# A two-layer block kernel: the rotary half-swap made by a TensorE matmul instead of by DMAs

## The reference, cut to what matters

```python
def apply_rope(x, cos, sin):
    x1, x2 = jnp.split(x.astype(jnp.float32), 2, axis=-1)
    c = cos[None, :, None, :]
    s = sin[None, :, None, :]
    return jnp.concatenate([x1 * c - x2 * s, x1 * s + x2 * c], axis=-1).astype(x.dtype)
```

## Time and profile before

| | us |
|---|---|
| median of 3 runs | 2912.36 (2909.82 to 2913.0) |
| the profiled execution, its own time | 2913.0 |
| its span, first to last instruction | 2911.2 |
| PE busy | 2748.0 (94%) |
| DVE busy | 1624.0 (56%) |
| ACT busy | 1092.4 (38%) |
| POOL busy | 608.6 (21%) |

### The profile page before, as it was taken

How to read it: one execution, slowest core, us unless ns; L and a number is a source line. 1 busy time by engine, 2 the same in 40 slices (tenths; PEclk the granted TensorE clock), 3 DMA queues, 4 the chain that set the end, 5 groups by cost and what they waited for, 6 DMA issues and landing times.

```text
span 2911.2 us, 36239 instructions
## 1 busy us (share of the span) xinstructions
PE 2748.0 (94%) x14752; PEld 2138.2 (73%) x14752; DVE 1624.0 (56%) x2752; ACT 1092.4 (38%) x1788; POOL 608.6 (21%) x338
## 2 busy tenths in 40 slices
PE   6999889999999998999998999989998999989997
PEld 5877568878878676788886888656676888756675
DVE  5779655554467674665456477744415247744424
ACT  3233633323232454433223563244313473244312
POOL 0000025776700000455450141000110131000110
PEclk8999989999999998999999999999999999999999
DMA  7353024454522111344442444211222223221222
GB/s 233 103 165 100 28 87 144 145 173 133 178 86 66 58 56 58 116 146 144 130 145 87 138 140 120 65 62 44 80 80 92 87 68 113 69 69 44 73 87 73
DMA packets 307462, 297.30 MB, mean 102 GB/s; under 512 B 9184, under 2 KB 300128, under 8 KB 307296
## 3 DMA queue, kind: packets, MB, share of 16 engines
q1 hardware_dynamic: 306048, 289.01, 31.6%
q0 software_dynamic: 960, 5.51, 0.5%
q10 hardware_dynamic: 288, 0.47, 0.0%
HBM read 284.73 MB, written 2.10 MB: 99 GB/s over the span
## 4 chain that ended last, share of the span: by engine, by line
PE 84%; DVE 6%; ACT 5%; POOL 2%; DMA 2%; issue 1%; DVEq 0%; ACTq 0%; SPq 0%; POOLq 0%
PE ps L516 83%; PE ps L699 2%; DVE wl L1266 1%; POOL raw L1729 1%; DMA raw<-in_w_in 1%; ACT wh L857 1%; DVE hl L1272 1%; DMA raw<-in_w_up 1%; DVE uv L1272 1%; POOL raw L1732 1%; POOL ug L1705 0%; DVE s L1528 0%; ACT recat L857 0%; DVE rawt L1272 0%; ACT s L857 0%
## 5 line engine op out<-in xcount | busy, mean ns | idle before, releaser
L516 PE MATMUL ps<-hh,wh 128*128 128x512 f32 x2288 | 933.0, 408 | 38.9 <-DVE hl L1272 26.1
L516 PE MATMUL ps<-hh,wl 128*128 128x512 f32 x2288 | 901.1, 394 | 0.0
L516 PE MATMUL ps<-hl,wh 128*128 128x512 f32 x2288 | 900.6, 394 | 0.0
L1266 DVE TENSOR_TENSOR wl<-raw,wh 128x2048 fp32r<-128x2048 f32 (+2 forms) x186 | 444.2, 2388 | 358.5 <-ACT wh L857 358.0
L516 PEld LDWEIGHTS ps<-hh,wh 128*128 128x128 f32 x2288 | 434.1, 190 | 166.9 <-issue 62.3
L516 PEld LDWEIGHTS ps<-hh,wl 128*128 128x128 f32 x2288 | 434.0, 190 | 95.9
L516 PEld LDWEIGHTS ps<-hl,wh 128*128 128x128 f32 x2288 | 435.2, 190 | 87.2 <-issue 4.3
L857 ACT ACTIVATE wh<-raw 128x2048 fp32r<-128x2048 f32 (+2 forms) x186 | 342.5, 1842 | 252.8 <-PE ps L516 134.1
L1729 POOL TENSOR_TENSOR raw<-raw,cond 128x2048 f32<-128x2048 f32 x40 | 182.2, 4555 | 252.5 <-DMA raw<-in_w_ada 252.5
L857 ACT ACTIVATE rawt<-ps 128x512 f32<-128x512 f32 (+1 forms) x106 | 63.3, 598 | 323.9 <-PE ps L516 323.8
L1732 POOL TENSOR_TENSOR raw<-raw 128x1024 f32<-128x1024 f32 x80 | 168.6, 2107 | 6.3
(11 more groups left out here) (229 smaller groups left out, 3812.8 us busy)
## 6 DMA issues: line engine op xcount, KB each, us to landing
raw<-in_w_in SPq DMA_DIRECT2D x74, 1024.0 KB, 5.5
raw<-in_w_ada SPq DMA_DIRECT2D x64, 1024.0 KB, 5.3
raw<-in_w_up SPq DMA_DIRECT2D x44, 1024.0 KB, 5.3
raw<-in_w_in SPq DMA_DIRECT2D x44, 512.0 KB, 5.1
raw<-in_w_out SPq DMA_DIRECT2D x16, 1024.0 KB, 5.4
raw<-in_w_down SPq DMA_DIRECT2D x16, 1024.0 KB, 5.4
stage<-in_w_ada SPq DMA_DIRECT2D x8, 1024.0 KB, 11.4
t1s<-rawt SPq DMA_DIRECT2D x124, 64.0 KB, 2.0
```

The costliest lines, as they stand in the source:

```text
L516: return e.matmul(o, a, b, start=start, stop=stop, skip_group_check=True)
L1266: return e.tensor_tensor(o, a, b, op)
```

## The change

The swap becomes a matmul with a constant 128x128 matrix of 0, 1 and -1. `rest` becomes a unit of PE too: it takes a bank of the main pool, waits for ACT's copy in `rawt`, and multiplies. The four DMAs of a tile and their waits on SP are gone, so that SP's program is a plain list of loads. POOL's product with `cos` now goes into `t1s`; DVE's product with `sin` reads the new PSUM bank and writes the destination, and the add follows. The constants grow by 128 columns (64 KB). The planner's table says that `rest` costs 0.9 on PE and then 1.4 on DVE, and this moves other work, as shown below the diff.

```diff
-C_ID, C_ONE, C_BLK, C_NTRI, C_NONE, C_CAUS, C_SWA, C_COS, C_SIN = (
-    0, 128, 256, 384, 512, 640, 768, 1024, 1536)
-C_W = 2048
+C_ID, C_ONE, C_BLK, C_ROT, C_NTRI, C_NONE, C_CAUS, C_SWA, C_COS, C_SIN = (
+    0, 128, 256, 384, 512, 640, 768, 896, 1152, 1664)
+C_W = 2176
...
-    "rope": (("ACT", 0.7, True), ("POOL", 1.3, False)), "rest": (("DVE", 1.5, True),), "v2": (("ACT", 0.4, True),),
+    "rope": (("ACT", 0.7, True), ("POOL", 1.3, False)), "rest": (("PE", 0.9, True), ("DVE", 1.4, True)), "v2": (("ACT", 0.4, True),),
...
-IN_MAIN_BANK = ("z", "q", "iv", "g", "qk", "a", "cqk", "v2", "rope", "bv", "gate", "mg", "br", "iw", "bvt")
+IN_MAIN_BANK = ("z", "q", "iv", "g", "qk", "a", "cqk", "v2", "rope", "bv", "gate", "mg", "br", "rest", "iw", "bvt")
...
-        elif unit[0] in ("iw", "bvt"):
+        elif unit[0] in ("rest", "iw", "bvt"):
...
+    def rest(l, nm, c):
+        dst, r = rope_of(M, nm, c)
+        b = take("main", ("rest", l, nm, c))
+        go.wait_ge(*at("rope_raw", l, nm, c))
+        mm(b[r, :], M.rot[r, r], M.rawt[X.slot["rope", l, nm, c]][r, :], True, True).then_inc(*up("pe_rest", ("rest", l, nm, c)))
...
-        raw_slot(("rope", l, nm, c), ("rope_cos", l, nm, c), ("rope_turned", l, nm, c))
+        raw_slot(("rope", l, nm, c), ("rope_cos", l, nm, c), ("rest", l, nm, c))
...
     def rest(l, nm, c):
         dst, r = rope_of(M, nm, c)
-        turned = M.t1s[X.slot.get(("rope", l, nm, c), 0)][r, :]
-        go.wait_ge(*at("rope_turned", l, nm, c))
-        tt(turned, turned, M.sin[r, :], ALU.mult).then_inc(*up("dve_rope"))
+        b, t1 = bank("rest", l, nm, c), M.t1s[X.slot.get(("rope", l, nm, c), 0)]
+        go.wait_ge(*at("rest", l, nm, c))
+        if nm == "bk":
+            go.wait_ge(*at("ts", l, 3, 3))
+        tt(dst, b[r, :], M.sin[r, :], ALU.mult).then_inc(*up("dve_rope", ("out", ("rest", l, nm, c))))
         go.wait_ge(*last("dve_rope"))
         go.wait_ge(*at("rope_cos", l, nm, c))
-        tt(dst, dst, turned, ALU.add).then_inc(*up("dve_rope", ("roped", l, nm, c), (
+        tt(dst, dst, t1[r, :], ALU.add).then_inc(*up("dve_rope", ("roped", l, nm, c), (
...
-        if nm == "bk":
-            go.wait_ge(*at("ts", l, 3, 3))
-        e.tensor_tensor(dst, M.rawt[X.slot.get(("rope", l, nm, c), 0)][r, :], M.cos[r, :], ALU.mult).then_inc(
-            *up("pool_rope", ("rope_cos", l, nm, c)))
+        if t1_free[n] is not None:
+            go.wait_ge(*at(*t1_free[n]))
+        t1_free[n] = ("roped", l, nm, c)
+        e.tensor_tensor(M.t1s[n][r, :], M.rawt[n][r, :], M.cos[r, :], ALU.mult).then_inc(*up("pool_rope", ("rope_cos", l, nm, c)))
...
-        for to in range(r.start, r.stop, 32):
-            src = to + 32 if to % 64 == 0 else to - 32
-            e.dma_start(M.t1s[n][to:to + 32, :], M.rawt[n][src:src + 32, :]).then_inc(*up16(f"turned_in{n}", ("rope_turned", l, nm, c)))
```

More of the change, by code:

```diff
@@ L147, in __init__ @@
         self.blk = cst[:, C_BLK:C_BLK + 128]
+        self.rot = cst[:, C_ROT:C_ROT + 128]
         self.caus = cst[:, C_CAUS:C_CAUS + 128]
@@ L1705, in up_value @@
         e.tensor_tensor(M.ug[ch % 4][:, :], M.ug[ch % 4][:, :], M.uv[ch % 3][:, :], ALU.mult).then_inc(*up("pool_gate", ("gated_f", l, ch)))
+    t1_free = [None, None]
     def rope(l, nm, c, c0, n, j):
[L1708 removed]
+        r = rope_of(M, nm, c)[1]
+        n = X.slot.get(("rope", l, nm, c), 0)
         go.wait_ge(*at("rope_raw", l, nm, c))
[L1710 to L1713 removed]
+        if t1_free[n] is not None:
+            go.wait_ge(*at(*t1_free[n]))
+        t1_free[n] = ("roped", l, nm, c)
+        e.tensor_tensor(M.t1s[n][r, :], M.rawt[n][r, :], M.cos[r, :], ALU.mult).then_inc(*up("pool_rope", ("rope_cos", l, nm, c)))
     def c_low(l, c, u):
@@ L1760, in sync_program @@
     M, T, up16, at, go, plan = X.M, X.T, X.tally.up16, X.tally.at, Go(e), X.plan
-    turned_free = [None, None]
     def first(n0, n1):
@@ L1766, in first @@
                 *up16(f"stage_in{n}", ("stage", n)))
-    def load(j, p):
+    xv = T["xT"].rearrange("(k p) s -> p k s", p=128)
+    for k in range(0, KD, 2):
+        e.dma_start(M.xT[:, k:k + 2, :], xv[:, k:k + 2, :]).then_inc(*up16(f"x_in{k}", ("loaded", "x", k // 2)))
+    first(0, 2)
+    for j, p in enumerate(plan):
         if j == 2:
@@ L1782, in load @@
             e.dma_start(view(M.raw[i]), src).then_inc(*up16(f"raw_in{i}", ("raw", j)))
-    def rope(l, nm, c):
-        n, r = X.slot.get(("rope", l, nm, c), 0), rope_of(M, nm, c)[1]
-        go.wait_ge(*at("rope_raw", l, nm, c))
-        if turned_free[n] is not None:
-            go.wait_ge(*at(*turned_free[n]))
-        turned_free[n] = ("roped", l, nm, c)
-        for to in range(r.start, r.stop, 32):
-            src = to + 32 if to % 64 == 0 else to - 32
-            e.dma_start(M.t1s[n][to:to + 32, :], M.rawt[n][src:src + 32, :]).then_inc(*up16(f"turned_in{n}", ("rope_turned", l, nm, c)))
-    xv = T["xT"].rearrange("(k p) s -> p k s", p=128)
-    for k in range(0, KD, 2):
-        e.dma_start(M.xT[:, k:k + 2, :], xv[:, k:k + 2, :]).then_inc(*up16(f"x_in{k}", ("loaded", "x", k // 2)))
-    first(0, 2)
-    loads, free = list(enumerate(plan)), {None}
-    while loads and loads[0][1]["raw_before"] in free:
-        load(*loads.pop(0))
-    for kind, *rest_ in X.order:
-        if kind == "rope":
-            rope(*rest_[:3])
-        elif kind in ("split", "ada", "adap") or kind == "br" and rest_[2] % 2:
-            free.add(rest_[-1])
-            while loads and loads[0][1]["raw_before"] in free:
-                load(*loads.pop(0))
     ov = X.out.rearrange("(k p) s -> p k s", p=128)
@@ L2286, in constants @@
     c[:, C_BLK:C_BLK + 128] = (i[:, None] // 64 == i[None, :] // 64)
+    r = np.zeros((128, 128), np.float32)
+    for o in range(128):
+        d = o % 64
+        if d < 32:
+            r[o + 32, o] = -1.0
+        else:
+            r[o - 32, o] = 1.0
+    c[:, C_ROT:C_ROT + 128] = r
     c[:, C_NTRI:C_NTRI + 128] = -(i[:, None] >= i[None, :]).astype(np.float32)
@@ L2294, in constants @@
     c[:, C_COS:C_COS + 512] = np.cos(ang)[np.arange(128) % 32]
-    c[:, C_SIN:C_SIN + 512] = np.sin(ang)[i % 32] * np.where(i % 64 < 32, -1, 1)[:, None]
+    c[:, C_SIN:C_SIN + 512] = np.sin(ang)[np.arange(128) % 32]
     m = np.zeros((128, 7, 128), np.float32)
```

3 lines of the change are left out of this document (1 added, 2 removed).

## The result

The changed kernel takes 2941.43 us (median of four runs, 2940.41 to 2946.04), the kernel before 2911.17 beside it (2909.82 to 2913.0). The ratio is 1.0108, with a 95% interval from 1.0092 to 1.0125: 30.3 us slower, where the prediction had 23.4 more and 2936 us, with a range from 2925 to 2946. The profiled execution of the changed kernel took 2948.6 us (span 2946.8), some 7 us above the median; the 21 executions on record lie between 2933.1 and 2951.1 us, with a median of 2942.1.

What follows compares the result with a forecast made beforehand. PE was taken to bound the rotary stretches; +28.8 swaps, -0.9 hidden bk swaps, +1.0 bank, 0 other engines, -6.0 planner, +0.5 index rounds gave +23.4 us. Forecast 2936 us in the median, range 2925 to 2946.

Steps and rivals of the forecast that it cites:

- the planner's -6.0: Tail of the mains: new planner costs leave 3 fewer uncovered steps of attention a; -6.0 us, bounds -3.3 and -7.5.
- The bound: Stretches with rotary tiles: PE is busy 20.00 of 20 us, so time is the sum of PE's work.
- The removal at nothing: 124 swap DMAs and the waits for them on DVE and SP: hidden by PE's work, so removal saves nothing.
- The rival of the queue: SP's queue: swaps held weight loads up for 116.5 us, so removing them makes it faster; about 2897 us, chance 0.04.
- The swaps at 0.90: PE in the rotary tiles: 32 added fp32 matmuls at 0.90 us each, +28.8 us, bounds 27.5 and 30.7.
- the bank term: Rotary tile boundaries: the next tile waits for ACT's copy to free its bank; +1 us in all, bounds 0 and 10.
- The rival of late copies: Rotary tile boundaries: bank waits uncovered because other ACT work precedes the copy; half of 30 give +15, about 2951 us, chance 0.14.
- One pass: Rival on the swap's price: each costs PE 0.23 us like a projection matmul, 7.4 for 32; about 2913 us, chance 0.02.
- Index rounds at +0.5: First layer: attention a's first step comes nearer the end of the index rounds; wait of 0 to 3 us, taken as 0.5.
- The rival of the cheaper tail: Tail: moved steps save their whole price, bk's swaps are hidden and the clock stays higher; about 2927 us, chance 0.11.
- the wait for DVE at nothing: Swap's own bank: DVE must have read it one tile earlier, with 5.4 us of cover; costed at nothing.

Runs made afterwards that it cites:

- e3: The changed kernel with each swap matmul issued twice into the same bank; 28.2 us more than the changed kernel.
- e6: The kernel before with the swap left out: no swap DMAs, DVE multiplies the unswapped tile by sin; +0.4 us against the kernel before.
- e2: The kernel before, swap still by DMA, with only the changed kernel's planner costs, so its new order; 2925.6 us.
- e11: e2 with two first-layer units of attention c moved back behind an adaptive chunk, a weight split and the first quarter of ik; 2918.0 us.
- e7: The changed kernel with a one-pass (fp32r) swap and the planner's old costs, so the order of the kernel before; 2930.5 us.
- e10: e7 (one-pass swap, old order) with the swap's bank taken from the side pool; 7.4 us faster than e7 in the medians.
- e1: The changed kernel, swap still a matmul, with the planner's old costs, so the units come in the order of the kernel before; 2943.8 us.
- e5: The changed kernel with three units moved in the finished order; first layer to the first branch matmul 253.0 us against 257.7, second-layer stretch 0.6 us longer.
- e9: e1 (fp32 swap, old order) with the swap's bank taken from the side pool; median 4.4 us under e1's.
- e4: The changed kernel with the swap as a one-pass (fp32r) matmul, ACT's copy rounding the tile; 2934.4 us.

## Why the prediction was right, point by point

The loss is 30.3 us where 23.4 was forecast. Nearly all of the difference is one term, the planner's -6.0: without it the sum is 29.4, against 30.3 measured. That the two are so close is partly luck, since gains and losses of the order cancel.

**The bound.** Right. PE sets the time in the stretches with rotary tiles: e3's second swap appears in full where PE had no wait (0.93 each in the second layer), e6's removed waits not at all.

**The removal at nothing.** Right, shown by e6. The condition belongs to it: with the order of before. In the order of e2 and e11 the same DMAs reached PE once, for 3.2 us, of which 2.6 are theirs by the changed kernel's 0.57. The rival of the queue is refuted by e6. That rival drew on the Trainium skill ("SBUF — State Buffer", the DMA setup cost): the latency of 2 us is in the earlier trace rows and cost nothing here.

**The swaps at 0.90.** Right in value, 0.87 without a tile behind and 0.96 with one. Half of the reason was missing. I had priced PE's passes and, apart from them, a copy that was just covered. The copy is in fact the later of the two wherever a tile follows directly, 11 places in the changed kernel with the spacings shown above. It ended 0.80 us after the swap's start, and the tile started at 0.85, where PE by itself could have begun its next matmul at 0.46. The prediction had PE want the bank after 0.86 us at the earliest. The loss is small, since that matmul would then have been spaced 0.64 and not 0.34: 0.09 each, 1.0 us in all. That this is the bank term of the sum is luck; the term was meant for copies that come late. The rival of late copies, 15 us, did not come, because ACT was at each tile in time.

**One pass.** The rival was wrong for this kernel, which has fp32. But its arithmetic, 7.4 us for 32 swaps, would have been wrong for a one-pass kernel too: e7 has +20.6. Only e10, which takes the copy's wait away as well, comes down toward it, with +13.1 in the median.

**The planner's move at -6.0.** This is the step that failed. It counted 3 steps fewer behind the last projection matmul, 4.0 us each, against 1.8 for a covered one, with bounds of -3.3 and -7.5. The changed kernel gained 0.6 us on e1 in the stretches and 2.4 in the medians, both outside these bounds. Three things were wrong.

- The count. In the second layer 6 score steps stand behind the last projection matmul (2640.72), at 2641.05, 2646.21, 2650.65, 2654.36, 2657.01 and 2660.50, not the 5 named above; so 2 steps moved and not 3.
- The worth of a step. The first layer's one step went with 2.7 to 4.5 us at like clocks. The second layer's gave nothing at like clocks, because a step that the new order puts between projections is not ready there: the split of a weight chunk that landed at 2625.12 stands in front of it on ACT (1.92 us) and on DVE (2.29), and PE waits 4.17 us with 12 projection matmuls queued behind. My 1.8 us came from a window where every step was ready.
- The place that was looked at. In the first layer the planner's new costs also moved two units of attention c ahead of an adaptive chunk. I had followed the order only where attention a stands; this lay 250 us earlier. e5 prices it at 4.7 us.

**Index rounds at +0.5.** No wait of PE for `sel` shows in the changed kernel; nothing contradicts the term, nothing measured it.

**The rival of the cheaper tail.** It fell with the same term. Its figures were wrong as well: by its own terms the sum is 23.4 - 1.5 - 0.9 - 4, so 2929 and not 2927, and the 16.02 us with the busy part at full clock would be 13.6 (11.58 x 0.79 + 4.44), not 12.

**One wait that I had not seen.** The planner's pool grows from two banks to three behind the last swap of the bq tiles. In the first layer the gate's tile so gets the bank that the swap before it has just filled, and waits until DVE has read it: 0.78 us at 1829.51, released by DVE `bq`, in the 20 us of the window shown above. The prediction had costed the wait for DVE at nothing with 5.4 us of cover, which holds at the other boundaries. e1 has the wait too (0.79), so it does not come of the new order; e9 and e10, with the swap in the side pool, do not have it.

The stretches, put together: 27.4 for the 30 swaps ahead of the gates, 0.8 for DVE's wait, 4.7 for the moved units of c, 0.8 for the waits of 0.42 and 0.57 less the 0.23 of before, 0.5 in the first layer that I can't name, and -0.1 for all behind the first branch matmul, where the swaps of bk, the moved steps and the clock cancel. That is 34.1 us in the profiles; the medians say 30.3. The profiled execution lies 7 us over its median, and which of these terms is smaller in the others stays open.

## What to carry to other kernels

- In this kernel an operation put on the bounding engine cost its time there in full, and what it replaced on other engines gave nothing, however long their waits looked. Between two limits that are nearly equal, here four passes and a copy that frees a bank, making one faster gains nothing until the other goes too.
- A cost in a planner's table changes the order everywhere, not only at the unit that it describes. Read the whole difference of the order, and ask at each moved unit what is queued behind it: here two units 250 us from the place that I watched cost 4.7 us, about what the moved steps gave. Look also at what runs beside the moved unit: here a POOL product came to stand beside a DVE split and took 2.70 us instead of 1.00.
- An order fits the work that it was made for: with the swap on PE this one was worth between nothing and some 2 us, and with the DMA swap it cost 15.

## What the runs showed of the hardware

- An fp32 matmul of 128x512 stands in the trace as two records. To the next matmul there are 0.46 us, but that one is spaced 0.64 from its own successor, where 0.23 is usual (e9). The true price, 0.87, only shows over both.
- ACT began its copy 0.43 us after the start of the tile's last matmul (2443.79 to 2444.22), and ended it 0.60 later, with four passes of PE between (the changed kernel) or one (e4). The bank was free 1.03 us after that start.
- The 64 KB swap DMAs, 2.0 us in the median, took 4.84 in e2 where the DMA engines had a share of 1.03, and 4.88 at the same place of e11.
- POOL's products of 128x384 took 1.00 us in the median. The four of the changed kernel that started beside a `wl` split of DVE took 1.71 to 2.73 and ended 0.86 to 0.89 us behind the split.
- The granted clock fell to a mean of 0.68 in the 10 us behind a PE wait of 1.38 us, and stayed at 1.00 in the same place of e5, where the wait was gone. A longer wait did not bring a longer slow stretch: behind the 4.17 us of the second layer the matmuls are spaced 0.43 up to 2635.42 and 0.23 from there. In the tails the clock was between 0.77 and 0.94, and behind a wait that was filled there it was lower in the next 30 us of e5 (0.68 against 0.94).
